# Expert gates of a routed layer spread by rounded products, and fewer first-layer products per routing head

## The reference, cut to what matters

```python
s1 = einsum("nhd,kd->nhk", q[:, :, 0], k1); s2 = einsum("nhd,kd->nhk", q[:, :, 1], k2)
v1, i1 = top_k(s1, 16); v2, i2 = top_k(s2, 16)              # 128 keys on each side
top_s, top_c = top_k((v1[..., :, None] + v2[..., None, :]).reshape(-1, 8, 256), 16)
expert = i1[top_c // 16] * 128 + i2[top_c % 16]
gate = softmax(top_s)
act = gelu(einsum("pd,ped->pe", x, u[expert]))
out = einsum("pe,ped->pd", gate * act, v[expert])
```

## Time and profile before

| what | value |
| --- | --- |
| median of 3 runs | 3946.09 us (3943.99 to 3948.16) |
| the profiled execution, its own time | 3945.7 us |
| its span, first to last instruction | 3943.8 us |
| TensorE matmul busy | 3745.4 us (95%) |
| VectorE busy | 2296.6 us (58%) |
| ScalarE busy | 1647.0 us (42%) |
| GpSimd busy | 1106.7 us (28%) |
| mean granted TensorE clock | 0.977 |

### The profile page before, as it was taken

The page is one execution under the profiler, slowest core; times in us unless marked ns, Lnnn a source line. Parts: engine busy times, 40 slices in busy tenths (PEclk is TensorE's granted clock), DMA queues, the critical chain, the costliest instruction groups (busy, mean ns, idle before and its releaser), DMA issues. The chain is left out here.

```text
span 3943.8 us, 47054 instructions
## 1 busy us (share of the span) xinstructions
PE 3745.4 (95%) x18172; PEld 3107.4 (79%) x18172; DVE 2296.6 (58%) x3601; ACT 1647.0 (42%) x2245; POOL 1106.7 (28%) x647
## 2 busy tenths in 40 slices
PE   7999899989999999999999999998999998789998
PEld 6888677768788888888888888886778886777886
DVE  6555445346366665755367777776555465855353
ACT  5555454445322234544444444445543223434222
POOL 1222122145144433333344444442020004502002
PEclk9999999899999999999999999999999999999999
DMA  4111021055234345345598888881123322132331
GB/s 178 55 53 54 12 66 47 13 187 203 68 126 131 129 128 192 123 185 201 205 297 264 265 267 264 267 259 60 35 74 103 96 96 65 32 99 75 97 96 64
DMA packets 226410, 515.87 MB, mean 131 GB/s; under 512 B 23792, under 2 KB 98800, under 8 KB 224016
## 3 DMA queue, kind: packets, MB, share of 16 engines
q1 hardware_dynamic: 203968, 408.89, 32.2%
q0 software_dynamic: 18720, 68.17, 5.3%
q10 hardware_dynamic: 3504, 35.85, 2.2%
HBM read 438.64 MB, written 69.21 MB: 129 GB/s over the span
## 5 line engine op out<-in xcount | busy, mean ns | idle before, releaser
L1330 PE MATMUL peer_banks<-peer_h_parts,peer_w_parts 128*128 128x512 f32 x3456 | 800.8, 392 | 8.5 <-DVE peer_w_parts L1785 5.1
L1330 PEld LDWEIGHTS peer_banks<-peer_h_parts,peer_w_parts 128*128 128x128 f32 x3456 | 646.5, 188 | 141.6 <-DVE peer_w_parts L1785 5.3
L1330 PE MATMUL peer_banks<-peer_act_parts,peer_w_parts 128*128 128x512 f32 x3072 | 696.8, 389 | 0.7 <-DVE peer_act_parts L1885 0.7
L1330 PEld LDWEIGHTS peer_banks<-peer_act_parts,peer_w_parts 128*128 128x128 f32 x3072 | 576.5, 188 | 120.8 <-DVE peer_w_parts L1890 1.1
L1529 POOL TENSOR_TENSOR peer_w_parts<-slots,peer_w_parts 128x1024 fp32r<-128x1024 f32 x142 | 339.9, 2394 | 579.7 <-ACT peer_w_parts L1676 579.7
L1330 PE MATMUL ffn_ps<-h_parts,ffn_w_parts 128*128 128x512 f32 x1920 | 450.7, 396 | 19.6 <-DVE h_parts L2495 11.0
L1676 ACT ACTIVATE peer_w_parts<-slots 128x1024 fp32r<-128x1024 f32 x272 | 287.0, 1055 | 386.0 <-PE peer_banks L1330 382.1
L1330 PEld LDWEIGHTS ffn_ps<-h_parts,ffn_w_parts 128*128 128x128 f32 x1920 | 364.9, 190 | 104.0 <-DVE ffn_w_parts L2339 15.6
L1330 PE MATMUL ffn_ps<-ffn_hidden,ffn_w_parts 128*128 128x512 f32 x1920 | 439.7, 391 | 2.3 <-DVE ffn_hidden L2402 2.3
L1330 PEld LDWEIGHTS ffn_ps<-ffn_hidden,ffn_w_parts 128*128 128x128 f32 x1920 | 361.5, 188 | 79.0 <-issue 3.9
L1880 DVE TENSOR_TENSOR peer_slab<-peer_slab 128x512 f32<-128x512 f32 x128 | 294.3, 2299 | 63.6 <-DMA peer_slab<-peer_gates 63.6
(11 more groups left out here) (553 smaller groups left out, 5447.3 us busy)
## 6 DMA issues: line engine op xcount, KB each, us to landing
slots<-in_peer_u SPq DMA_DIRECT2D x128, 512.0 KB, 3.6
slots<-in_peer_v SPq DMA_DIRECT2D x128, 512.0 KB, 4.8
slots<-in_mlp_w SPq DMA_DIRECT2D x128, 512.0 KB, 3.5
peer_slab<-in_w_mod POOLq DMA_DIRECT2D x96, 512.0 KB, 4.2
peer_acts<-h SPq DMA_DIRECT2D x128, 256.0 KB, 2.4
peer_gates<-peer_slab ACTq DMA_DIRECT2D x16, 2048.0 KB, 16.6
peer_slab<-peer_acts SPq DMA_DIRECT2D x128, 256.0 KB, 5.2
peer_slab<-peer_gates SPq DMA_DIRECT2D x128, 256.0 KB, 5.5
```

The costliest lines, as they stand in the source:

```text
L1330: last = nc.tensor.matmul(out, w(a, k), x(b, k), start=start and k == ks[0] and n == 0, stop=stop and k == ks[-1] and n == 2)
```

## The change

Each head makes three u tiles in place of six, and a u tile now follows every group of tokens, so 24 u tiles move from stage 1 to stage 3; their number and the number of query tiles stay. The product of a token is no longer one fp32 matmul of 128 x 128. ScalarE rounds the gates once to `gate_hi` (float32r); VectorE computes `lo_share` = (gate - gate_hi) / gate_hi for all tokens (a subtraction, a maximum, a reciprocal and a product of 128 x 512); `cols` has two halves per token: VectorE writes one-hot times `gate_hi` into the first (eight instructions per group as before), and GpSimd writes the first times `lo_share` into the second (`share`, one 128 x 1024 instruction per group). TensorE makes one float32r matmul of 128 x 256 per token. A group's output is handled in two halves of four tokens, m = 2g and 2g + 1, in three buffers of two banks. For each half ScalarE copies the part of the rest to SBUF (`lo_sb`, 128 x 512), and VectorE adds it to the high part in PSUM and writes the sum into `slab` with the step of 128 (`add`, 128 x 512). VectorE's order is now the two adds of group g, then `cols` and `rows` of group g + 2. GpSimd's queue becomes: `share` of the next group, then the low part of one tile, in turn. In the last group of a block ScalarE handles the u tile before it issues the slab's DMAs.

```diff
-U_HEAD = 6
+U_HEAD = 3
-        cols = ph.sb("cols", [P, 2, G, NKEY])
+        cols = ph.sb("cols", [P, 2, G, 2, NKEY], F32R)
+        gate_hi = ph.sb("gate_hi", [P, T], F32R)
...
+        def g_ps(m):
+            at = (2 + 2 * (m % 3)) * T
+            return banks[:, at:at + HG * 2 * P]
...
         def between(g):
 
-            return g % 8 in (0, 1, 3, 4, 6)
+            return True
@@ GpSimd
-            for p in range(2, FRONT):
+            def low(p):
                 g.wait_ge(w_hi, p + 1)
                 nc.gpsimd.tensor_tensor(wp[:, p % 2, 1, :], ring.raw[:, p % R, :], wp[:, p % 2, 0, :].bitcast(F32),
                                         ALU.subtract).then_inc(w_lo, 1)
+
+            def share(n):
+                b = n % 2
+                g.wait_ge(cols_done, n + 1)
+                nc.gpsimd.tensor_tensor(cols[:, b, :, 1, :], cols[:, b, :, 0, :].bitcast(F32),
+                                        lo_share[:, n * G:(n + 1) * G].unsqueeze(2).to_broadcast([P, G, NKEY]),
+                                        ALU.mult).then_inc(cols_lo, 1)
...
+            g.wait_ge(share_ready, 1)
+            share(0)
+            for tt in range(TT):
+                for i in range(groups):
+                    at = tt * groups + i
+                    if at + 1 < TT * groups:
+                        share(at + 1)
+                    if between(i):
+                        if u_place(n) + 2 < FRONT:
+                            low(u_place(n) + 2)
+                        n += 1
...
@@ TensorE
                 pe.wait_ge(rows_done, g + 1)
-                pe.wait_ge(cols_done, g + 1)
-                if g >= 2:
-                    pe.wait_ge(g_stored, g - 1)
-                for t in range(G):
-                    last = nc.tensor.matmul(g_ps[:, b * 1024 + t * P:b * 1024 + (t + 1) * P], rows[:, b, t, :], cols[:, b, t, :],
-                                            start=True, stop=True)
-                last.then_inc(g_done, 1)
+                pe.wait_ge(cols_lo, g + 1)
+                for m in (2 * g, 2 * g + 1):
+                    if m >= 3:
+                        pe.wait_ge(g_stored, m - 2)
+                    for j in range(HG):
+                        t = m % 2 * HG + j
+                        last = nc.tensor.matmul(g_ps(m)[:, j * 2 * P:(j + 1) * 2 * P], rows[:, b, t, :],
+                                                cols[:, b, t].rearrange("p a i -> p (a i)"), start=True, stop=True)
+                    last.then_inc(g_done, 1)
@@ ScalarE
+                for m in (2 * g, 2 * g + 1):
+                    act.wait_ge(g_done, m + 1)
+                    if m >= 2:
+                        act.wait_ge(g_stored, m - 1)
+                    A(lo_sb[:, m % 2], g_ps(m).rearrange("p (t a i) -> p t a i", t=HG, a=2)[:, :, 1, :], ACT.Copy).then_inc(lo_read, 1)
...
+            act.wait_ge(tr_stored, 3)
+            A(gate_hi[:], selt[:, 2, :], ACT.Copy).then_inc(share_hi, 1)
@@ VectorE
+            dve.wait_ge(share_hi, 1)
+            hi = gate_hi[:].bitcast(F32)
+            st.then(V.tensor_tensor(lo_share, selt[:, 2, :], hi, ALU.subtract))
+            st.then(V.tensor_scalar(selt[:, 2, :], hi, 1.0e-30, None, ALU.max))
+            st.then(V.reciprocal(selt[:, 2, :], selt[:, 2, :]))
+            V.tensor_tensor(lo_share, lo_share, selt[:, 2, :], ALU.mult).then_inc(share_ready, 1)
...
+            form(0)
+            form(1)
+            for g in range(TT * groups):
+                add(2 * g)
+                add(2 * g + 1)
+                if g + 2 < TT * groups:
+                    form(g + 2)
```

More of the change, by code:

```diff
@@ L1412, in peer @@
         stage = K.h[:, 0:4, :]
-        rows = K.h[:, 4:8, :].rearrange("p (b x) t -> p b (x t)", b=2).rearrange("p b (g i) -> p b g i", g=G)
+        rows = K.h_rounded[:, 4:8, :].rearrange("p (b x) t -> p b (x t)", b=2).rearrange("p b (g i) -> p b g i", g=G)
+        HG = G // 2
         flat = slab[:].rearrange("p i t -> p (i t)")
@@ L1530, in _ @@
                                         ALU.subtract).then_inc(w_lo, 1)
+            def share(n):
[4 more added lines that the diff above has]
+                                        ALU.mult).then_inc(cols_lo, 1)
+            n = EARLY + AHEAD
+            for p in range(2, u_place(n - 1) + 3):
+                low(p)
+            g.wait_ge(share_ready, 1)
[9 more added lines that the diff above has]
+                        n += 1
+                for j in range(TAILS[tt]):
+                    if u_place(n) + 2 < FRONT:
+                        low(u_place(n) + 2)
+                    n += 1
             g.wait_ge(slab_out[2], 16 * TT)
@@ L1650, in _ @@
                     if n == 0 and k == 2:
-                        pe.wait_ge(g_stored, TT * groups)
+                        pe.wait_ge(g_stored, 2 * TT * groups)
                     if n == 0 and k == 6:
@@ L1740, in _ @@
                     if g == groups - 1:
-                        act.wait_ge(g_stored, (tt + 1) * groups)
+                        up(n)
+                        n += 1
+                        act.wait_ge(g_stored, 2 * (tt + 1) * groups)
                         for s in range(4):
@@ L1744, in _ @@
                                           flat[:, s * quarter:(s + 1) * quarter]).then_inc(slab_out[s], 16)
-                    if between(g):
+                    elif between(g):
                         up(n)
@@ L1861, in _, with form, add @@
             dve.wait_ge(tr_stored, 3)
-            for g in range(TT * groups):
+            dve.wait_ge(share_hi, 1)
[4 more added lines that the diff above has]
+            V.tensor_tensor(lo_share, lo_share, selt[:, 2, :], ALU.mult).then_inc(share_ready, 1)
+            def form(g):
                 b = g % 2
                 if g >= 2:
-                    dve.wait_ge(g_done, g - 1)
+                    dve.wait_ge(g_done, 2 * (g - 1))
+                for t in range(G):
+                    one = slice(g * G + t, g * G + t + 1)
+                    last = V.tensor_scalar(cols[:, b, t, 0, :], iota[:], selt[:, 1, one], gate_hi[:, one].bitcast(F32),
+                                           ALU.is_equal, ALU.mult)
+                last.then_inc(cols_done, 1)
                 V.tensor_tensor(rows[:, b], iota[:].unsqueeze(1).to_broadcast([P, G, NKEY]),
                                 selt[:, 0, g * G:(g + 1) * G].unsqueeze(2).to_broadcast([P, G, NKEY]), ALU.is_equal).then_inc(rows_done, 1)
[L1868 to L1871, removed]
+            def add(m):
+                dve.wait_ge(lo_read, m + 1)
+                if m >= 2 * groups and m % (2 * groups) == 0:
+                    for s in slab_out:
+                        dve.wait_ge(s, 16 * (m // (2 * groups)))
+                at = m % (2 * groups) * HG
+                both = g_ps(m).rearrange("p (t a i) -> p t a i", t=HG, a=2)
+                V.tensor_tensor(slab[:, :, at:at + HG].rearrange("p i t -> p t i"), both[:, :, 0, :], lo_sb[:, m % 2],
+                                ALU.add).then_inc(g_stored, 1)
+            form(0)
[5 more added lines that the diff above has]
+                    form(g + 2)
             def weigh(n):
```

5 lines of the change are left out of this document (4 added, 1 removed).

## The result

The changed kernel takes **3966.66 us** (median of 5 runs, 3966.03 to 3969.19) against 3945.98 (3943.99 to 3948.16) of the kernel before on the same chip: the ratio is 1.0054, with a 95% interval of 1.0042 to 1.0067. It is slower by 21 us, where 69 were forecast; 3966.66 lies inside the range of 3940 to 4100, but the loss is 0.3 of the one forecast. The profiled executions differ by as much, 3964.7 against 3943.8 us of span.

A forecast was written before the change was run, and what follows sets the result against it. The prediction took TensorE's queue to bound the heads and the spreading. Its terms, -54 + 88 + 14 + 16 + 5 = +69 us on 3945.7, gave 4015 us; own range 3980 to 4052, wider range 3940 to 4100.

The forecast's parts named there:

- Gate products: Spreading: eight float32r products per group take 0.96 us instead of 1.81, -54 us of TensorE's queue over 64 groups.
- rival of a narrower product that is not cheaper: Gate products: weights dominate a 256-column matmul, so no saving per token; some 4035 us; chance 0.03.
- Pace of the groups: Spreading: mutually excluding VectorE and GpSimd instructions make late groups take 8.0 us against TensorE's 6.40, +88 us over four blocks.
- Adds: Spreading: VectorE's two adds per group, 0.7 to 1.2 us each, run beside GpSimd and are costed at nothing.
- rival of uncovered adds: Spreading: adds ahead of the next columns stretch each slow group by 1.4 to 2.4 us; 4091 to 4145 us; chance 0.12.
- Columns going free: Rival for the spreading: float32r columns no longer exclude GpSimd, TensorE sets the pace; 3933 us (3915 to 3950); chance 0.15.
- Start of the spreading: Between transposes and first gate product: the chain from gate_hi to the share delays TensorE to 21.8 from 7.3 us, +14 us.
- Heads: Heads with 24 tiles fewer: VectorE becomes the bound, GpSimd encounters cost 2 us per head, transposes come later, +16 us.
- Clock: After TensorE's two pauses of about 16 and 14 us the granted clock falls, 2.3 us of work each, +5 us.

The follow-up runs named there:

- order alone: Kernel before the change with three u tiles per head and one behind every group, fp32 products kept: 3976.74 us, ratio 1.0080.
- the share on ScalarE: Changed kernel with the product by lo_share moved from GpSimd to ScalarE, as eight 128 x 128 copies per group: 3939.65 us, ratio 0.9984.
- The share twice: Changed kernel with GpSimd's product by lo_share done twice per group, writing the same values: 4075.21 us, ratio 1.0330.
- the two other orders: Two runs on the changed kernel: VectorE forms rows before columns, 3983.25 us; ScalarE makes the high part before the gelu in the spreading, 3983.31 us.
- The rounding one tile earlier: Changed kernel with ScalarE rounding the gates to gate_hi before it waits for the tile TensorE makes meanwhile: 3959.95 us, ratio 1.0042.
- four tiles per head: Changed kernel with four u tiles per head in place of three, and 6, 6, 6, 9 behind the blocks: 3934.26 us, ratio 0.9967.
- taking GpSimd's work away: Changed kernel with GpSimd's low part of the heads' 40 tiles covering 8 of 1024 columns, waits and matmuls kept: 3939.97 us, ratio 0.9983.
- The products alone: Changed kernel with six u tiles per head and one behind five of eight groups, as before the change: 4067.42 us, ratio 1.0314.

## Why the prediction was right in direction and wrong in size

**Gate products, right.** The eight products take 0.94 to 1.02 us, forecast 0.96, and where TensorE sets the pace they save 53 us (order alone against the share on ScalarE), forecast 54. The rival of a narrower product that is not cheaper is refuted.

**Pace of the groups, wrong in size: +88 forecast, +26 to +27 measured.** The failed step is the sum of the instructions that exclude each other, "7.8, and with 0.2 for some four hand-overs 8.0 us". The mechanism was right: the columns that write float32r are held up as before.

```profile
L1914 DVE TENSOR_SCALAR peer_cols<-peer_iota,peer_selt,peer_gate_hi x512: 324/336/2040, 1366.5 to 1929.7; 128x128 fp32r<-128x128 f32 x171
L1544 POOL TENSOR_TENSOR peer_cols<-peer_cols,peer_sel x64: 1888/1898/2810, 1368.8 to 1933.4; 128x1024 fp32r<-128x1024 f32 x64
L1927 DVE TENSOR_TENSOR peer_slab<-peer_banks,peer_sel x128: 1044/1096/1122, 1374.5 to 1938.2; 128x512 f32<-128x512 f32 x128
```

These are lines of the changed kernel with min/median/max ns. The share takes 1.90 us where I took 2.2: the sum becomes 7.48. The hand-overs don't add 0.2 but take 0.6 off, to 6.88. How a hand-over goes is seen on the first column instruction and on the first two together, in the timeline of the slow group:

```profile
1439.86 0.56 DVE L1914 TENSOR_SCALAR peer_cols<-peer_iota,peer_selt,peer_gate_hi 128x128 fp32r<-128x128 f32 x1
1439.86 2.42 DVE L1914 TENSOR_SCALAR peer_cols<-peer_iota,peer_selt,peer_gate_hi 128x128 fp32r<-128x128 f32 x2
```

The second ends at 1442.28, 0.08 us after the share (1440.30 + 1.90), where one takes 0.34 undisturbed: it looks as if a blocked instruction has spent its lead time when the other ends. The first ends at 1440.42, 0.08 us behind the low part (1436.87 + 3.47). The same holds for the low part behind rows: 2.27 us from the end of rows (1438.07) to its own end, for 2.39. Since TensorE needs 6.42, an error of 1.1 us in a sum of 8 is one of 70% in the difference that is paid: 0.46 us instead of 1.6, over 55 groups. That is the lesson on the size: the loss was a small difference between two large sums, and its range had to be as wide as the error of both. Mine held 7.8 to 8.4, with nothing below the bare sum, though no row of before showed three or four hand-overs in a row. The share twice, the two other orders and the share on ScalarE carry this reading. That blocked instructions save their lead time is read from the timelines, not tried by itself. The forecast also had the place of the share wrong: it put it beside the adds, but the low part, ready when the rows are formed, comes first and takes that cover, and the share stands in the columns.

**Adds, right.** 1.10 us each, beside GpSimd, at constant length; the rival of uncovered adds is refuted. What covers them is the low part and not, as forecast, the share. By the Trainium skill ("SBUF — State Buffer", the note on cachelines) every access to a new 16-byte line pays; the trace agrees, with 1.10 us at a step of 128 elements against 0.68 contiguous, though these are two different instructions and no run here changes the step alone.

**Columns going free, refuted.** The float32r columns are held up like the old ones, 2040 ns for one that takes 336. By the Trainium skill ("SBUF — State Buffer", the part on SBUF's two separate sides) whichever of the two engines starts first has the shared ports for its whole instruction; the trace agrees, with 1.94 us for the second column instruction beside the share's 1.90.

**Start of the spreading, right.** +16.6 for +14 and 2.3 of clock: the chain from the rounding (1358.95) to the first product took 12.72 us, where my terms add up to 12.7 (the prediction has 12.9). The reciprocal took 3.35 us; my 3 was a guess between 0.7 and 5.6, and that it came so close is luck. The subtraction took 2.34 with its blocking, and the pause was 14.2. The rounding one tile earlier won 6.7 us of it.

**Heads, wrong in size: +16 forecast, +29.4 measured.** The step that failed is "five open instructions of 128 x 1024 per head": I took the small ones as free of GpSimd. VectorE's lines of the heads, mean ns and idle time before them:

```profile
L1884 DVE TENSOR_TENSOR peer_slab<-peer_slab,peer_iota 128x1024 f32<-128x1024 f32 x16 | 28.8, 1801 | 0.5
L1886 DVE TENSOR_TENSOR peer_slab<-peer_slab 128x1024 f32<-128x1024 f32 x16 | 25.8, 1614 | 0.6
...
L1872 DVE CAST peer_slab<-peer_slab 128x64 f32<-128x64 uint32 x16 | 11.4, 713 | 0.6
...
L1877 DVE TENSOR_TENSOR peer_sel<-peer_slab 128x64 f32<-128x64 f32 x8 | 4.1, 518 | 0.3
L1882 DVE CAST peer_slab<-peer_slab 128x128 f32<-128x128 uint32 x8 | 3.9, 488 | 0.3
```

A cast of 64 elements (L1872) takes 195 ns unhindered and 713 on average here, 2371 at most: a short instruction can be held up for as long as a long one. Whether it is depends on the phase: in the kernel before and with four tiles per head, where TensorE's scores start every head, none of the 16 casts was held up (195 to 197 ns), although GpSimd was busy for 42% of the heads there and 39% here. The stretches come to 28 us in all, 3.5 per head for my 2, and taking GpSimd's work away won 26.7 us. The +29.4 are 20.1 us of waiting before the transposes, 7.4 in two waits for the cast L1872, which the forecast did not have, and slower work behind these.

**Clock, right.** Behind the two long pauses the work takes about 2.7 us longer each (transposes and tile 2.47 and 7.19 us for 1.29 and 5.72; 9.11 us to the next products for 6.42), 5 forecast for both; the small waits within the slow groups left the granted clock at 1.00 in the spreading. The products alone show what pauses of 5 us do, 20 of them: 41 us.

The two errors have opposite signs, about -61 and +13, and the first decides. The forecast "slower" rested on the right reasons.

## What to carry to other kernels

Where two engines exclude each other, write one lap of the busier engine as a sequence and ask which of the other's instructions stands beside work that is exempt; in the orders tried here the lap grew by the uncovered one alone, and the order of the queues decided whether that was the long one or the short one. Before a saving on the bounding engine is counted, set its new period against that lap, with an error bar on the difference and not on the sums. Work that is added to relieve the bounding engine belongs on an engine that holds up no other: the same product on ScalarE won back what it had cost on GpSimd. And where tiles cover another engine's work, take only as many as leave TensorE the longer side: one tile more in each head closed both kinds of wait there.

## What the runs showed of the hardware

- A product on GpSimd with a broadcast operand takes 1.90 us for 1024 elements, a subtraction of two plain operands 2.39.
- ScalarE's copy with a scale per partition takes 2.45 us for eight of 128 elements, 0.31 each: longer than the 1.90 on GpSimd, but VectorE's columns and adds keep their length beside it (2.10 and 2.05 us).
- The reciprocal on VectorE takes 353 ns for 32 elements and 3353 for 512: (3353 - 353) / 480 = 6.25 ns per element between the two.
- A column instruction blocked by GpSimd ends about 0.1 us after GpSimd's.
- An add that reads PSUM and SBUF keeps its length beside GpSimd's low part (1044 to 1122 ns in all 128).
- Behind pauses of TensorE of 5.1 to 5.8 us the next products take 2.04 us for 1.10, which is its lower clock; behind pauses of 0.2 to 0.3 us nothing changes. Behind pauses of 2.0 to 2.2 us (the share twice) both happen: granted clock 0.59 over 1406.56 to 1410.00, with products of 1.53 us, and 1.18 us at other groups.
